# The end of the last layer on one core: token tiles finished one by one, statistics of three tiles on ScalarE, the last tile's closing operation in two halves

## The reference

```python
h = layer_norm(DEEPNORM_ALPHA * x + heads @ w_o, ln1_g, ln1_b)
ffn = (jax.nn.silu(h @ w_gate) * (h @ w_up)) @ w_down
return layer_norm(DEEPNORM_ALPHA * h + ffn, ln2_g, ln2_b)

def layer_norm(x, g, b):
    mu = jnp.mean(xf, axis=-1, keepdims=True)
    var = jnp.mean(jnp.square(xf - mu), axis=-1, keepdims=True)
    return ((xf - mu) * lax.rsqrt(var + LN_EPS) * g + b).astype(x.dtype)
```

## Time and profile before

| | |
|---|---|
| median of 3 runs | 1997.35 us (1996.68, 1997.35, 2002.61) |
| time of the profiled execution | 2000.51 us |
| its span, first to last instruction | 1998.6 us |
| TensorE busy | 1937.0 us, 97% of the span |
| VectorE, ScalarE, GpSimd busy | 799.0, 827.2, 702.1 us |
| last matmul starts | 1984.87 us |
| last VectorE operation | 1994.27 us, for 1.28 us |

### The profile page before, as it was taken

The page is one execution under the profiler, slowest core; times in us unless marked ns, Lnnn a source line. Parts: engine busy times, 40 slices in busy tenths (PEclk is TensorE's granted clock), DMA queues, the critical chain, the costliest instruction groups (busy, mean ns, idle before and its releaser), DMA issues.

```text
span 1998.6 us, 26892 instructions
## 1 busy us (share of the span) xinstructions
PE 1937.0 (97%) x10454; PEld 1637.8 (82%) x10454; DVE 799.0 (40%) x1830; ACT 827.2 (41%) x1571; POOL 702.1 (35%) x552
## 2 busy tenths in 40 slices
PE   8999999989999999999999999999999999999997
PEld 4898889877788888877888888888887898888885
DVE  3555556442546435476511111017367551111004
ACT  3221268355238446577233222125477533223211
POOL 1523312125452135310544454445321245444452
PEclk9999999999999999999999999999999999999999
DMA  9544311112331124310333333322420223333321
GB/s 278 172 161 145 136 43 44 28 47 85 106 128 42 34 65 129 89 54 22 85 100 90 106 86 126 106 77 91 122 80 23 63 65 106 106 86 104 127 84 43
DMA packets 198117, 183.72 MB, mean 92 GB/s; under 512 B 31686, under 2 KB 166204, under 8 KB 197992
## 3 DMA queue, kind: packets, MB, share of 16 engines
q1 hardware_dynamic: 191960, 170.67, 27.7%
q10 hardware_dynamic: 6032, 11.33, 1.8%
HBM read 179.86 MB, written 5.40 MB: 93 GB/s over the span
## 4 chain that ended last, share of the span: by engine, by line
PE 84%; DVE 7%; ACT 3%; issue 2%; POOL 2%; DMA 1%; SPq 0%; ACTq 0%; DVEq 0%
PE ps L1302 23%; PE ps L1304 23%; PE ps L1303 23%; PE ps L1391 3%; PE ps L1809 2%; PE ps L1886 2%; POOL w_lo L722 2%; PE ps L1358 1%; PE ps L1377 1%; PE ps L1904 1%; PE ps L1421 1%; DVE sc L2465 1%; ACT w_hi L776 1%; PE ps L1336 1%; DVE qc L2496 1%
## 5 line engine op out<-in xcount | busy, mean ns | idle before, releaser
L722 POOL TENSOR_TENSOR w_lo<-raw,w_hi 128x512 fp32r<-128x512 f32 (+1 forms) x518 | 680.3, 1344 | 1193.0 <-ACT w_hi L776 1192.9
L776 ACT ACTIVATE w_hi<-raw 128x1024 fp32r<-128x1024 f32 (+2 forms) x261 | 258.7, 1037 | 265.2 <-PE ps L1304 203.8
L1302 PE MATMUL ps<-g_hi,w_lo 128*128 128x512 f32 (+1 forms) x928 | 348.4, 375 | 1.5 <-POOL w_lo L722 1.5
L1303 PE MATMUL ps<-g_lo,w_hi 128*128 128x512 f32 (+1 forms) x928 | 347.5, 374 | 0.0
L1304 PE MATMUL ps<-g_hi,w_hi 128*128 128x512 f32 (+1 forms) x928 | 347.5, 374 | 0.0
L1302 PEld LDWEIGHTS ps<-g_hi,w_lo 128*128 128x128 f32 x928 | 174.7, 188 | 33.8 <-issue 1.7
L1304 PEld LDWEIGHTS ps<-g_hi,w_hi 128*128 128x128 f32 x928 | 174.7, 188 | 31.3
L1303 PEld LDWEIGHTS ps<-g_lo,w_hi 128*128 128x128 f32 x928 | 174.7, 188 | 30.9
L1302 PE MATMUL ps<-h_hi,w_lo 128*128 128x512 f32 (+1 forms) x496 | 180.3, 364 | 4.0 <-DVE h_lo L2027 2.3
L2591 DVE TENSOR_TENSOR tmp_f<-ps,tmp_f 128x512 f32<-128x512 f32 x44 | 30.4, 692 | 370.7 <-PE ps L1304 370.7
L1304 PE MATMUL ps<-h_hi,w_hi 128*128 128x512 f32 (+1 forms) x496 | 174.6, 352 | 0.0
(11 more groups left out here) (283 smaller groups left out, 3466.4 us busy)
## 6 DMA issues: line engine op xcount, KB each, us to landing
raw<-in_w_in SPq DMA_DIRECT2D x30, 1024.0 KB, 5.1
raw<-in_w_mod SPq DMA_DIRECT2D x24, 1024.0 KB, 6.9
raw<-in_w_gate SPq DMA_DIRECT2D x44, 512.0 KB, 4.0
raw<-in_w_up SPq DMA_DIRECT2D x44, 512.0 KB, 5.2
raw<-in_w_down SPq DMA_DIRECT2D x22, 1024.0 KB, 4.9
raw<-in_w_out SPq DMA_DIRECT2D x8, 1024.0 KB, 5.0
strips<-bias_rows ACTq DMA_DIRECT2D x18, 256.0 KB, 3.7
raw<-in_w_in SPq DMA_DIRECT2D x16, 256.0 KB, 4.4
```

Source lines behind the costliest of these rows:

```text
L722: pool.tensor_tensor(w_lo[:, i % SPLIT, a:e], raw_of(what)[:, a:e], w_hi[:, i % SPLIT, a:e].bitcast(F32), ALU.subtract).then_inc(s_tile_lo ...
L776: act.activation(w_hi[:, i % SPLIT, a:b], raw_of(what)[:, a:b], ACT.Copy).then_inc(s_tile_hi.sem, s_tile_hi.nth((what, n)))
L1302: pe.matmul(o, lhs[1], rhs[0], start=first, stop=False)
L1303: pe.matmul(o, lhs[0], rhs[1], start=False, stop=False)
```

## The change

In the last layer alone, TensorE walks the last two weight tiles by `tile_by_tile()`: (0,0) (1,0) (0,1) (1,1) (2,0) (2,1) (3,0) (3,1). For tiles 0 to 2 ScalarE makes mean and variance (`last_spread`): a copy of the row with a sum, the sum times -1/D, a square of the centred row with a sum, the root of that over D plus epsilon. VectorE leaves `bn_stats`, `bn_aggr` and the addition of epsilon out for these tiles, and its order over the tiles is another. Tile 3 keeps the statistics on VectorE. Its last operation is cut in two halves of 512 columns, each stored by a DMA of its own. In every `norm`, of both layers, the operation with the mean now stands ahead of the reciprocal. GpSimd sets a constant tile `eps_c` at the program's start.

```diff
+            def last_spread(y, t):
+                if t == 0:
+                    act.wait_ge(s_eps.sem, s_eps.at(0))
+                    act.wait_ge(s_mm.sem, s_mm.at((y, "ffup", FC - 1)))
+                else:
+                    act.wait_ge(s_root.sem, s_root.at((y, 2, t - 1)))
+                act.wait_ge(s_resid.sem, s_resid.at((y, 2, 1, t)))
+                act.activation(spread[:], res[:, t, :], ACT.Copy, accum_out=centre[:, t, 0:1]).then_inc(s_centre.sem, s_centre.nth((t, 0)))
+                act.wait_ge(s_centre.sem, s_centre.at((t, 0)))
+                act.activation(centre[:, t, 1:2], centre[:, t, 0:1], ACT.Copy, scale=-1.0 / D).then_inc(s_centre.sem, s_centre.nth((t, 1)))
+                act.wait_ge(s_centre.sem, s_centre.at((t, 1)))
+                act.activation(spread[:], res[:, t, :], ACT.Square, bias=centre[:, t, 1:2], accum_out=ssq[:, t:t + 1]).then_inc(s_centre.sem, s_centre.nth((t, 2)))
+                act.wait_ge(s_centre.sem, s_centre.at((t, 2)))
+                act.activation(rstd[:, t:t + 1], ssq[:, t:t + 1], ACT.Sqrt, bias=eps_c[:], scale=1.0 / D).then_inc(s_root.sem, s_root.nth((y, 2, t)))
...
-                    root((y, 2, t), t, 1)
+                    if l + 1 < DEPTH or t == XT - 1:
+                        root((y, 2, t), t, 1)
+                    else:
+                        last_spread(y, t)
...
-                for t, i in paired():
+                for t, i in paired() if l + 1 < DEPTH else tile_by_tile():
...
                 def norm(n, w, done, t):
+                    dve.wait_ge(s_ln.sem, s_ln.at((y, n)))
+                    if (n, l) == (2, DEPTH - 1) and t < XT - 1:
+                        dve.wait_ge(s_root.sem, s_root.at((y, n, t)))
+                        step(V.scalar_tensor_tensor(res[:, t, :], res[:, t, :], centre[:, t, 1:2], w[:, 0, :], ALU.add, ALU.mult))
+                    else:
+                        step(V.scalar_tensor_tensor(res[:, t, :], res[:, t, :], mean_var[:, t, 0:1], w[:, 0, :], ALU.subtract, ALU.mult))
                     inverse((y, n, t), t, 1)
-                    dve.wait_ge(s_ln.sem, s_ln.at((y, n)))
-                    step(V.scalar_tensor_tensor(res[:, t, :], res[:, t, :], mean_var[:, t, 0:1], w[:, 0, :], ALU.subtract, ALU.mult))
-                    V.scalar_tensor_tensor(res[:, t, :], res[:, t, :], rstd[:, t:t + 1], w[:, 1, :], ALU.mult, ALU.add).then_inc(done.sem, done.nth((y, t)))
+                    if (n, l, t) == (2, DEPTH - 1, XT - 1):
+                        for half in range(2):
+                            c = slice(512 * half, 512 * half + 512)
+                            V.scalar_tensor_tensor(res[:, t, c], res[:, t, c], rstd[:, t:t + 1], w[:, 1, c], ALU.mult,
+                                                   ALU.add).then_inc(done.sem, done.nth((y, t, half)))
+                    else:
+                        V.scalar_tensor_tensor(res[:, t, :], res[:, t, :], rstd[:, t:t + 1], w[:, 1, :], ALU.mult,
+                                               ALU.add).then_inc(done.sem, done.nth((y, t)))
...
-                for t in range(XT):
+                if l + 1 == DEPTH:
+                    for t in range(XT):
+                        for ch in range(2):
+                            residual(2, ch, t, (y, "down", FC // 2 - 1, ch, t), 2 * t + ch, t == XT - 1)
+                        if t == 1:
+                            norm(2, ln2, s_x_final, 0)
+                            norm(2, ln2, s_x_final, 1)
+                    statistics(2, XT - 1)
+                    norm(2, ln2, s_x_final, 2)
+                    norm(2, ln2, s_x_final, 3)
+                for t in range(XT if l + 1 < DEPTH else 0):
```

More of the change, by code:

```diff
@@ L171, in _program @@
         lam_c = put("lam_c", [P, 2])
+        eps_c = put("eps_c", [P, 1])
+        centre = put("centre", [P, XT, 2])
         lam = put("lam", [P, 8])
@@ L271, in _program @@
         tmp_f = at("tmp_f", [P, 4, SEQ], ao2_at)
+        spread = at("spread", [P, D], names["g_hi"][0])
         rr = at("rr", [A_HEADS + B_HEADS, SEQ + P], uf_at)
@@ L353, in _program @@
         s_causal = Signal(nc, ctx, seen, "causal")
+        s_centre = Signal(nc, ctx, seen, "centre")
+        s_eps = Signal(nc, ctx, seen, "eps")
         s_sub = Signal(nc, ctx, seen, "sub")
@@ L704, in _ @@
                     sp.dma_start(res_c[:], I["ctx"][0].rearrange("(t p) d -> p t d", p=P)).then_inc(s_x_landed[2].sem, 16)
-            for t in range(XT):
+            for t in range(XT - 1):
                 sp.wait_ge(s_x_final.sem, s_x_final.at((2 * DEPTH - 1, t)))
                 sp.dma_start(out[0, P * t:P * t + P, :], res[:, t, :]).then_inc(s_stored.sem, 16)
-            sp.wait_ge(s_stored.sem, 16 * XT)
+            for half in range(2):
+                a = 512 * half
+                sp.wait_ge(s_x_final.sem, s_x_final.at((2 * DEPTH - 1, XT - 1, half)))
+                sp.dma_start(out[0, P * (XT - 1):P * XT, a:a + 512], res[:, XT - 1, a:a + 512]).then_inc(s_stored.sem, 16)
+            sp.wait_ge(s_stored.sem, 16 * (XT + 1))
         @block.gpsimd
@@ L713, in _ @@
             pool.memset(ones[:], 1.0).then_inc(s_ones.sem, s_ones.nth(0))
+            pool.memset(eps_c[:], LN_EPS).then_inc(s_eps.sem, s_eps.nth(0))
             pool.memset(wf[:], 0.0).then_inc(s_wf_zero.sem, s_wf_zero.nth(0))
@@ L1324, in turn_rows, with tile_by_tile @@
                     m.then_inc(turned.sem, turned.nth((y, t, g)))
+            def tile_by_tile():
+                return [(0, 0), (1, 0), (0, 1), (1, 1), (2, 0), (2, 1), (3, 0), (3, 1)]
             def paired():
@@ L2555, in _, with residual @@
                     lo_part(g_lo[:, CHUNKS.index(k), :], ps[:, n % 4, :], g_hi[:, CHUNKS.index(k), :], (y, "m", k), (y, "m", k))
-                def residual(n, ch, t, key, bank):
+                def residual(n, ch, t, key, bank, counted=True):
                     dve.wait_ge(s_mm.sem, s_mm.at(key))
@@ L2561, in residual @@
                     V.scalar_tensor_tensor(x_, x_, ALPHA, ps[:, bank, :], ALU.mult, ALU.add).then_inc(s_resid.sem, s_resid.nth((y, n, ch, t)))
-                    dve.wait_ge(s_resid.sem, s_resid.at((y, n, ch, t)))
-                    step(V.bn_stats(bn[:, t, ch, :], x_))
+                    if counted:
+                        dve.wait_ge(s_resid.sem, s_resid.at((y, n, ch, t)))
+                        step(V.bn_stats(bn[:, t, ch, :], x_))
                 def statistics(n, t):
@@ L2569, in norm @@
                 def norm(n, w, done, t):
-                    inverse((y, n, t), t, 1)
-                    dve.wait_ge(s_ln.sem, s_ln.at((y, n)))
-                    step(V.scalar_tensor_tensor(res[:, t, :], res[:, t, :], mean_var[:, t, 0:1], w[:, 0, :], ALU.subtract, ALU.mult))
-                    V.scalar_tensor_tensor(res[:, t, :], res[:, t, :], rstd[:, t:t + 1], w[:, 1, :], ALU.mult, ALU.add).then_inc(done.sem, done.nth((y, t)))
+                    dve.wait_ge(s_ln.sem, s_ln.at((y, n)))
[4 more added lines that the diff above has]
+                        step(V.scalar_tensor_tensor(res[:, t, :], res[:, t, :], mean_var[:, t, 0:1], w[:, 0, :], ALU.subtract, ALU.mult))
+                    inverse((y, n, t), t, 1)
+                    if (n, l, t) == (2, DEPTH - 1, XT - 1):
+                        for half in range(2):
+                            c = slice(512 * half, 512 * half + 512)
[4 more added lines that the diff above has]
+                                               ALU.add).then_inc(done.sem, done.nth((y, t)))
                 for t in range(XT):
```

## The result

| | before | changed |
|---|---|---|
| median (9 runs each) | 2002.18 us (1996.68 to 2004.17) | 2007.53 us (2005.28 to 2010.78) |
| profiled execution: time, span | 2000.51, 1998.6 | 2005.28, 2003.4 |
| ratio, with 95% interval | | 1.0038 (1.0026 to 1.0050) |

The change makes the kernel 0.38% slower, about 7.6 us. The forecast was 1993.7 us, 0.19% faster. The kernel before was also measured more often than the three runs on which the forecast stood, and its median rose from 1997.35 to 2002.18 us. The runs of one kernel fall into two groups some 6 us apart, so a median can jump from one to the other and the quotient of two medians (here 1.0027) is not the ratio given; the ratio is what counts, and its interval, 1.0026 to 1.0050, is 5 to 10 us.

The account below looks back on a forecast made before the run. TensorE was taken to bound the kernel, with VectorE filling the 13.3 us behind its last matmul. Gains of 2.7 + 0.5 + 0.5 = 3.7 us off the median of 1997.35 gave 1993.7 us, range 1991.2 to 1997.3.

Parts of the forecast that it names:

- The step that failed: Whole kernel: TensorE's end is fixed by its work, and the new constant and `spread` lie in memory nobody waits for.
- The slower rival: Last layer: copy and square not in the root's table, so tiles 1 and 2 switch there and back; 1998.4 us, chance 0.04.
- Part 1: Last layer's norm: statistics of three tiles leave VectorE for ScalarE, VectorE ends at 1992.85 against 1995.55; 2.7 us gained.
- ScalarE's chain: Last layer, per tile: copy, scaling, square, root and four hand-overs take 3.00 us; tile 0 adds a 1.28 us table load.
- The upper bound: Last layer, ScalarE's work per tile: 3.8 us at most, if each of four hand-overs costs 0.27 us.
- The longer-chain rival: Last layer: ScalarE waits for itself at more than 0.04 us, or the table load costs more; 1995.0 us, chance 0.14.
- the extra time at a switch: ScalarE's table load at tile 0: by the skill page a drain of about 1380 ns more, making the sum 1.3 us later.
- The load's price: Last layer, tile 0: the 1.28 us table load stands behind work waiting for VectorE and counts in full.
- At 2.8 the gain is 2.8: Last layer: with 2.8 us per tile on ScalarE instead of 3.00, the gain is 2.8 us instead of 2.7.
- tile 2's second half is earlier by 1.36 x 3 = 4.1 us: Last layer, TensorE's new order: only tile 2 comes earlier than before, its second half by 4.1 us.
- Part 2: Kernel's end: only 256 KB instead of 512 KB stored behind the last operation; 0.5 us gained, between 0 and 0.65.
- Part 3: Layer 0's closing norm: the wide operation hides the root's wait, tiles 0 and 1 save 0.25 each; 0.5 us, 0 to 0.7.

Follow-up runs that it names:

- b_shift64: The kernel before with `res` and every tile behind it moved by 64 bytes: 2011.34 us, ratio 1.0047.
- b_shift128: The kernel before with `res` and every tile behind it moved by 128 bytes: 2028.48 us, ratio 1.0130.
- b_shift32: The kernel before with `res` and every tile behind it moved by 32 bytes: 2030.56 us, ratio 1.0135.
- b_hid64: The kernel before with only `hid_hi` and `hid_lo` moved by 64 bytes: 2004.17 us, ratio 1.0025.
- b_wlo64: The kernel before with `w_lo` moved by 64 bytes, `res` and all tiles behind it by 256: 2020.54 us, ratio 1.0100.
- a_end: The changed kernel with `eps_c` and `centre` put at the end of the memory, behind all other tiles: 1996.90 us, ratio 0.9977 to the kernel before.
- a_early: `a_end` with one more root of a column, so that ScalarE's table is loaded early: 1994.13 us, ratio 0.9984 to the kernel before.
- a_round256: The changed kernel with the offset rounded up to a multiple of 256 bytes before `res`: 1996.03 us, ratio 0.9971 to the kernel before.
- b_all64: The kernel before with every tile moved by 64 bytes, the weight tiles too: 2003.93 us, ratio 1.0012.
- b_shift256: The kernel before with `res` and every tile behind it moved by 256 bytes: 2003.02 us, ratio 1.0005.

## Why the prediction was wrong, point by point

**The step that failed.** The prediction priced the new tiles at nothing: "The constant at the start and the unused result `spread` lie in memory that nobody waits for", and ahead of that, "TensorE's end is fixed by its work". It asked who waits for the new tiles and not what they push. `spread` lies inside a tile that was there and pushes nothing; `eps_c`, and `centre`, which the prediction does not mention, pushed every tile behind them by 64 bytes against the weight tiles, and TensorE's work took longer. In the profiled executions TensorE's last matmul moved from 1984.87 to 1992.98, 8.1 us later. The profiled execution of the kernel before had also lost time that the changed one did not. The busy time by stretch (the clock is the number ahead of the DMA share) in the 20 us in which the clock fell, before and after:

```profile
290.00:310.00 20.00, 17.79 (x110) 17.08 (x110) 10.23 (x39) 14.27 (x30) 5.01 (x4) 0.74 0.00 1
```

```profile
290.00:310.00 20.00, 19.05 (x146) 18.13 (x144) 13.27 (x52) 16.59 (x36) 7.79 (x6) 0.91 0.17 54
```

A mean clock of 0.74 is about 10 us at the lower level, 1.2 GHz, and 0.91 is about 3.6. Half of that time is lost at most, since TensorE is not busy throughout, so the kernel before had lost up to 3.4 us more. I estimate from this that the pace cost 8.1 to 11.5 us. Less the 3.3 us that the end gained this leaves 4.8 to 8.2; the ratio says 7.6, with an interval of 5 to 10.

A sum over all starts gives somewhat more, and shows what this net loss is made of. In the changed kernel the distances between matmuls over 512 columns with a weight tile sum to 18.5 us more than before, but those over 256 columns to 5.4 us less (more on them at the end), so 13.1 us in all. In the same way the starts of `b_shift64` give 13.2 us, of `b_shift128` 29.3, of `b_shift32` 29.5, of `b_hid64` 7.0 and of `b_wlo64` 21.8, where the times say 9.4, 26.6, 28.6, 5.0 and 20.4. So the pace is enough for each loss; the 1 to 4 us that the sums lie above the times are taken up elsewhere, and I did not follow where. The sums also say why 64 bytes cost so little beside 32 and 128: the matmuls whose row names the weight tile second, those of the gate and up products among them (3404 of 5386 over 512 columns), are then 229 ns apart and not 232 or 233, and those over 256 columns gain most.

None of the rivals was this one. The slower rival was a table load per tile, and it did not happen.

**Part 1, VectorE and ScalarE, 2.7 us.** Right in its mechanism and nearly in size. In the profile of `a_end`, where the pace is that of before, the last matmul starts 10.42 us ahead of the span's end, against 13.75 before: 3.3 us, for the 3.2 forecast of parts 1 and 2 together. VectorE runs from 1967.51 to 1989.99, 22.48 us, where 1992.85 - 1970.33 = 22.52 was forecast. This does not test the terms of ScalarE: tile 3's arrival sets the end, in the prediction's steps as in the trace. These are its rows that answer to the earlier trace rows:

```profile
1967.51 0.69 DVE L2595 SCALAR_TENSOR_TENSOR res<-res,ps 128x512 f32<-128x512 f32 x1 [102.50 <-PE ps L1334]
...
1974.06 1.29 DVE L2609 SCALAR_TENSOR_TENSOR res<-res,centre,ln 128x1024 f32<-128x1024 f32 x1 [1.78 <-ACT rstd L811]
...
1988.58 1.41 DVE L2616 SCALAR_TENSOR_TENSOR res<-res,rstd,ln 128x512 f32<-128x512 f32 x2
```

**ScalarE's chain, 3.00 us plus 1.28.** From the changed kernel's timeline of ScalarE:

```profile
1980.22 1.06 ACT L804 ACTIVATE spread<-res 128x1024 f32<-128x1024 f32 x1 [7.20 <-DVE res L2594]
1981.19 0.18 ACT L804 ACTIVATION_READ_ACCUMULATOR spread<-res 128x1 f32 x1
1981.40 0.20 ACT L806 ACTIVATE centre<-centre 128x1 f32<-128x1 f32 x1
1981.64 1.15 ACT L808 ACTIVATE spread<-res,centre 128x1024 f32<-128x1024 f32 x1
1982.70 0.18 ACT L808 ACTIVATION_READ_ACCUMULATOR spread<-res,centre 128x1 f32 x1
1982.90 1.28 ACT L810 ACT_TABLE_LOAD   x1
1984.19 0.29 ACT L810 ACTIVATE rstd<-ssq,eps_c 128x1 f32<-128x1 f32 x1
...
1987.22 0.29 ACT L810 ACTIVATE rstd<-ssq,eps_c 128x1 f32<-128x1 f32 x1
```

Roots 0 and 1 are 3.03 us apart. ScalarE's wait for itself costs 0.02 to 0.04 us (1981.19 + 0.18 to 1981.40), the value taken. (The upper bound was mis-added: 3.00 with four waits of 0.27 for 0.04 is 3.9, not 3.8.) The longer-chain rival is refuted. So is the extra time at a switch: the sum's read ends at 1982.88, the load starts at 1982.90, and the root 1.29 us later. The Trainium skill, page "ScalarE: Activation LUTs", section "What ACT_TABLE_LOAD costs", adds a drain of about 1380 ns to each switch; here, as in the trace before, no row shows it.

**The load's price at the end.** The prediction said that it "counts in full". It does at tile 0 and for the root of tile 1. At the end of the kernel it is worth nothing, as `a_early` shows: without it VectorE waits for tile 3, and tile 3's arrival is TensorE's. The prediction's own steps said so: VectorE is ready for tile 3 at 1983.83, which arrives at 1983.93, so earlier roots are worth nothing. "At 2.8 the gain is 2.8" is wrong by this; it stays 2.7. Wrong too, without weight in the sum, is that tile 2's second half is earlier by 1.36 x 3 = 4.1 us. By the order of the pairs both of its halves come two steps of six matmuls earlier, 2.7 us.

**Part 2, the last store, 0.5 us.** From the end of VectorE's last operation to the end of the span: 1998.6 - 1995.55 = 3.05 us before, 1992.5 - 1989.99 = 2.5 in `a_end`. Right.

**Part 3, the other norms, 0.5 us.** TensorE's wait for VectorE's norm of tile 1 in layer 0 (0.54 us ahead of L1323) is gone, and its wait for GpSimd's low part shrank. The view of waits of `a_end`, 1325:1382, answers to the earlier trace rows:

```profile
PE ps L1332 <- POOL w_lo L733: 2.2, 4, 1.3
PEld ps L1353 <- DVE res L2619: 0.4, 1, 0.4
```

2.6 became 2.2. Together 0.9 us at this place. How much of it reaches the end is not separated from the scatter: `a_end` and `a_round256` are 4.6 and 5.8 us faster by their ratios, with intervals of 2 us to each side, and 3.3 + 0.5 to 0.9 lies within both. So the 0.5 is neither shown nor refuted.

**The range and the chances.** With the distances kept, the changed kernel's ratio of 0.9977 agrees with the 0.9981 that was forecast, within the interval. What was forecast is what the edits do. What was measured is what the edits do and what their 64 bytes do.

## What to carry to other kernels

Ask of every new tile not only who uses it but which tiles stand behind it. In a kernel bound by TensorE, compare the addresses of the matmuls' operands before and after, and if a small tile must go in, put it at the end or round the offset up so that the distances stay. (That a distance kept is the best one is not shown: see the matmuls over 256 columns below.) When a change in one corner makes the whole kernel slower, count instructions in equal stretches of both traces: TensorE's busy share and clock looked the same here, 267 and 259 matmuls in 60 us did not.

## What the runs showed of the hardware that was not expected

The pace of matmuls over 512 columns of split float32 depends on the distance in bytes between their operands' tiles in memory. In the layouts tried it is 227 ns with distances that are a multiple of 256; with 32, 64 or 128 off it is 229 to 233 ns, 1 to 3% slower, at the same granted clock. All addresses moved together by 64 bytes cost nothing. The Trainium skill, page "SBUF — State Buffer", section "Operand start alignment", asks only that an operand starts at a multiple of its element size, which every one of these layouts does, and says that this is about legality and not speed; the runs show that layouts which that rule allows are not equally fast.

The same 64 bytes make matmuls over 256 columns faster. The busy time by stretch in one of layer 1's products, 256 columns wide, before and in the changed kernel:

```profile
1401.50:1411.50 10.00, 10.00 (x85) 10.00 (x85) 9.31 (x14) 7.98 (x13) 5.05 (x4) 1.00 0.19 51
```

```profile
1403.50:1413.50 10.00, 10.00 (x90) 10.00 (x90) 9.11 (x14) 7.88 (x13) 5.05 (x4) 1.00 0.20 54
```

That is 90 matmuls in 10 us for 85, 113.5 ns apart for 119.9; `b_shift64` has 113.5 there too, `b_all64` and `b_shift256` 119.9. So a multiple of 256 bytes is the best of the distances tried for 512 columns, and not for 256. Why the two widths differ is not known.

Which operands meet, and where, stays open. Moving `w_lo` alone lengthened all three intervals and cost more than moving everything by 64 bytes, so it is not a matter of one matmul's own pair. What was not tried: other types than split float32, a distance of 192 bytes or under 32, and whether some other distance would be faster than 227 ns for 512 columns.
